# Late attention: gated tiles written over the gates by VectorE and split by GpSimd two maps behind its scaling

## The chip, the cores and the metric

The kernel runs on one core of a Trainium2 chip. The metric is the device time of one execution, in microseconds. A core has five engines that run their own instruction streams and wait for each other by semaphores: TensorE (PE in the profile, with its weight loads as PEld), VectorE (DVE), ScalarE (ACT), GpSimd (POOL) and SyncE (SP, which issues DMAs). TensorE writes to PSUM; GpSimd works on SBUF here.

## The reference

Two transformer blocks follow each other on a sequence of 512 tokens with model width 1024. The first block has windowed and sparse attention, a gated merge and a convolutional feed-forward layer. The change lies in the second block, which mixes three kinds of attention, gates their concatenated output with silu(z), and projects it:

```python
def second_block(x, mem, positions, norm_g, w_in, ...):
    for l in range(DEPTH):
        lam_init = 0.8 - 0.6 * math.exp(-0.3 * l)
        h = rms_norm(x, norm_g[l])
        proj = h @ w_in[l]
        cq, ckv, kr, dq, dk, dv, mq, z = jnp.split(proj, IN_OFFSETS_2, axis=-1)
        y_mla = mla_branch(cq, ckv, kr, positions, ...)      # 8 heads, causal, 64 wide
        y_diff = diff_branch(dq, dk, dv, positions, ...)     # 4 heads, each a difference of two softmaxes
        y_mem = mem_branch(mq, mem, ...)                     # 4 heads over 256 memory tokens
        y = jnp.concatenate([y_mla, y_diff, y_mem], axis=-1) * jax.nn.silu(z)
        x = x + y @ w_out[l]
    return x

# in mla_branch, for a block of 128 queries
sc = jnp.einsum('bqhd,bkhd->bhqk', qblk, k).astype(jnp.float32) * scale
sc = jnp.where(causal_mask(start, s)[None, None], sc, NEG_INF)
p = jax.nn.softmax(sc, axis=-1).astype(v.dtype)
return jnp.einsum('bhqk,bkhd->bqhd', p, v)

# in diff_branch
a = (p[:, :, 0] - lam * p[:, :, 1]).astype(v.dtype)
o = rms_norm(o, subln_g) * (1.0 - lam_init)
```

Everything is float32. The dense products are done as three products of a high part (rounded to the format that TensorE takes at full rate, `fp32r`) and a low part (what the rounding lost): high by high, high by low, low by high. So each operand of a dense product needs a high and a low tile, and this holds for the gated output `y` as well.

## The kernel before

The kernel is one program: projections and the first attention ("ab"), merge, feed-forward layer and its output product, the projections of the second block with their norms, then the late attention, and last the output product `wout2`. Weights arrive in units of 128x1024; for each, ScalarE writes the high part (`stream`, line 731) and GpSimd the low part (`low_half`, line 652).

The late attention works through a list of 20 maps, `LATE`. A map is one softmax matrix of one head (512 queries by its keys) with a place i from 0 to 19:

```text
 0 mla0   1 mla1   2 diff0 hold  3 diff0 sub   4 mla2   5 mla3   6 diff1 hold  7 diff1 sub   8 mla4
 9 diff2 hold  10 diff2 sub  11 mla5  12 diff3 hold  13 diff3 sub  14 mla6  15..18 mem0..mem3  19 mla7
```

Every engine has its own loop over i, and each loop handles several maps in one turn, at different stages. For one map the stages are these.

- TensorE, `scores`: products of queries and keys into PSUM.
- VectorE, `biased` (line 1324): adds the causal mask, copies to SBUF, takes the row minimum. Its inputs are one tile of PSUM and one of SBUF.
- ScalarE (line 889): exponentials with row sums. They need the table of the exponential on ScalarE; another function needs its own table, brought in by a table load instruction.
- VectorE, `normed`: reciprocals of the sums (line 1337), then the rows are scaled, in three groups by 128-query blocks: block 1, blocks 0 and 2, block 3. VectorE scales the first two groups (line 1364). GpSimd scales block 3 of every mla map (`widest`, line 669), half of every mem map (line 715), and all four blocks of a "hold" map (line 709). In a "sub" map VectorE computes the difference with the held map (line 1362), after a small product with lambda (line 1348).
- TensorE, `turn` (line 1987): transposes of the scaled rows, group by group; ScalarE copies them to SBUF (line 864).
- TensorE, `values` (line 2010): products with the values, into PSUM bank 6 or 7 in turn. They wait until the output before the last has left its bank.

For a finished mla or mem map (12 of them, 64 rows by 512 queries each) the end is: VectorE multiplies the output in PSUM by the gate in `FX` and writes it back to PSUM (line 1440, semaphore `y_f`); ScalarE copies that to SBUF, which rounds it to the high part (line 933, `y_hi`); one turn later VectorE subtracts to get the low part (line 1247, `y_lo`). The diff outputs take another way, through a norm over each head: it needs a square root on ScalarE (line 851, which waits for `dm_rin`, VectorE's reciprocal at line 1445), a gating on VectorE (lines 1388 and 1391), a copy on ScalarE (line 917) and the low part on VectorE.

Order on each engine is program order. `wout2` multiplies the eight gated tiles in the order 4, 5, 6, 7, 0, 1, 2, 3 (4 and 5 are diff, 6 mem0 and mem1, 7 mem2 and mem3, 0 to 3 mla), each with its own wait in the first unit.

## Time and profile before

| | |
|---|---|
| median of three runs | 1101.36 us (1101.25 to 1102.08) |
| profiled execution, its own time | 1101.32 us |
| span of the profile | 1099.5 us |
| busy in the span | PE 1050.5, PEld 870.7, DVE 622.8, ACT 550.8, POOL 436.9 us |
| first 950 us | PE busy 919.30 us, granted clock 0.99 |
| 950 to 1052.5 us, the late attention | PE busy 87.41 us, granted clock 0.93 |
| 1052.5 us to the end, `wout2` | PE busy 43.77 of 47.00 us, granted clock 1.00 |

The profile is one execution. Busy time of an engine is the time in which it had an instruction running. The chain of waits is followed back from the last instruction, at each step to what released it; an engine that isn't on it there had time to spare. A timeline gives an engine's instructions by start. Groups by form give, for one line and shape, how often it ran and the mean time of one. A window's row gives busy times with instruction counts, and the granted clock of TensorE, where 1.00 is 2.4 GHz and 0.50 is 1.2 GHz.

### The profile page before, as it was taken

Reading aid. Unit: us, or ns where it says so; the run is one execution under the profiler, and the core shown is the slowest. Engines: PE = TensorE matmul, PEld = TensorE weight load, DVE = VectorE, ACT = ScalarE, POOL = GpSimd, SP = SyncE. Lnnn points to the kernel's source line nnn. Section 1 sums busy time; section 2 is a strip of 40 time slices with the busy share of each in tenths; the row PEclk is TensorE's granted clock in tenths of the full one; section 3 lists DMA queues with packets and bytes.
Section 4 is the critical chain, followed back from the end, with each engine's and each line's share of the span. In section 5 each row is a group of like instructions: output and inputs, shape, how many; then the busy total and the mean of one; then the engine's idle time right before and its main releaser. Section 6 shows DMA issues by size and latency. Waiting matters only on the chain.

```text
span 1099.5 us, 15072 instructions
## 1 busy us (share of the span) xinstructions
PE 1050.5 (96%) x5086; PEld 870.7 (79%) x5086; DVE 622.8 (57%) x1414; ACT 550.8 (50%) x1143; POOL 436.9 (40%) x227
## 2 busy tenths in 40 slices
PE   6999999999999999999999999999999979899798
PEld 3779888799888788888888888778887868766577
DVE  4557376988745466454545455442225989586732
ACT  5443465777634344444444444443344374888831
POOL 2356222233324444444444444414444244444332
PEclk9999999999999999999999999999999999898999
DMA  7564221111013322222223233233353224332123
GB/s 257 186 174 144 74 76 58 58 40 39 29 58 117 128 100 96 96 96 95 100 93 104 93 106 134 96 134 100 112 178 101 77 71 140 98 94 77 49 77 114
DMA packets 38811, 111.87 MB, mean 102 GB/s; under 512 B 5235, under 2 KB 8563, under 8 KB 38067
## 3 DMA queue, kind: packets, MB, share of 16 engines
q1 hardware_dynamic: 28572, 87.60, 24.4%
q10 hardware_dynamic: 8584, 18.89, 5.3%
q0 software_dynamic: 1600, 4.66, 1.1%
q8 instruction: 32, 0.52, 0.2%
q14 instruction: 23, 0.19, 0.1%
HBM read 100.25 MB, written 7.96 MB: 98 GB/s over the span
## 4 chain that ended last, share of the span: by engine, by line
PE 36%; issue 35%; POOL 12%; DVE 8%; ACT 4%; DMA 3%; POOLq 0%; ACTq 0%; DVEq 0%
POOL WLO L652 11%; PE PS L1813 8%; PE PS L1815 8%; PE PS L1814 8%; PE PS L1987 2%; PE PS L2010 2%; DMA RAW<-wstream 2%; PE PS L1901 1%; PE PS L1946 1%; PE PS L1947 1%; DVE PB L1324 1%; ACT PB L889 1%; ACT WHI L731 1%; PE PS L2149 1%; DMA X<-xT 1%
## 5 line engine op out<-in xcount | busy, mean ns | idle before, releaser
L652 POOL TENSOR_TENSOR WLO<-RAW,WHI 128x1024 fp32r<-128x1024 f32 x147 | 355.7, 2420 | 529.1 <-ACT WHI L731 528.8
L731 ACT ACTIVATE WHI<-RAW 128x1024 fp32r<-128x1024 f32 x154 | 162.8, 1058 | 294.4 <-PE PS L1815 273.5
L1813 PE MATMUL PS<-HHI,WHI 128*128 128x512 f32 x648 | 257.4, 397 | 10.6 <-DVE HLO L1225 9.2
L1814 PE MATMUL PS<-HLO,WHI 128*128 128x512 f32 x648 | 254.1, 392 | 0.0
L1815 PE MATMUL PS<-HHI,WLO 128*128 128x512 f32 x648 | 253.9, 392 | 0.0
L1813 PEld LDWEIGHTS PS<-HHI,WHI 128*128 128x128 f32 x648 | 122.9, 190 | 39.9 <-issue 11.7
L1813 PE MATMUL PS<-BHI,WHI 128*128 128x512 f32 x368 | 145.3, 395 | 3.2 <-POOL WLO L652 1.8
L1815 PE MATMUL PS<-BHI,WLO 128*128 128x512 f32 x368 | 143.4, 390 | 0.0
L1815 PEld LDWEIGHTS PS<-HHI,WLO 128*128 128x128 f32 x648 | 122.8, 189 | 26.0
L1814 PE MATMUL PS<-BLO,WHI 128*128 128x512 f32 x368 | 143.3, 389 | 0.0
L1814 PEld LDWEIGHTS PS<-HLO,WHI 128*128 128x128 f32 x648 | 123.0, 190 | 25.4 <-issue 0.8
L1207 DVE TENSOR_TENSOR PS<-PS,PB 128x512 f32<-128x512 f32 x63 | 43.9, 696 | 87.0 <-PE PS L1815 85.4
L1247 DVE TENSOR_TENSOR BLO<-PS,BHI 128x256 fp32r<-128x256 f32 (+4 forms) x140 | 64.8, 508 | 39.4 <-ACT BHI L923 27.9
L1813 PEld LDWEIGHTS PS<-BHI,WHI 128*128 128x128 f32 x368 | 69.1, 188 | 20.4 <-POOL WLO L652 2.5
L889 ACT ACTIVATE PB<-PB,ST 128x256 f32<-128x256 f32 (+4 forms) x164 | 79.4, 500 | 4.8 <-DVE ST L1324 4.7
L1815 PEld LDWEIGHTS PS<-BHI,WLO 128*128 128x128 f32 x368 | 69.1, 188 | 14.8
L1814 PEld LDWEIGHTS PS<-BLO,WHI 128*128 128x128 f32 x368 | 69.1, 188 | 13.8
L1536 DVE SCALAR_TENSOR_TENSOR FX<-PS,CL,FX 128x511 f32<-128x511 f32 (+1 forms) x88 | 61.7, 742 | 12.0 <-ACT FX L983 11.8
L1813 PE MATMUL PS<-WHI,HHI 128*128 128x512 f32 (+2 forms) x128 | 48.5, 379 | 2.7 <-ACT PB L1009 2.0
L1987 PE MATMUL PS<-IDN,PB 128*128 128x128 f32 x270 | 39.3, 284 | 11.5 <-DVE PB L1364 4.8
L1815 PE MATMUL PS<-WHI,HLO 128*128 128x512 f32 (+2 forms) x128 | 48.2, 376 | 0.0
L1814 PE MATMUL PS<-WLO,HHI 128*128 128x512 f32 (+2 forms) x128 | 47.9, 374 | 0.0
(322 smaller groups left out, 1646.0 us busy)
## 6 DMA issues: line engine op xcount, KB each, us to landing
RAW<-wstream SPq DMA_DIRECT2D x154, 512.0 KB, 3.2
X<-xT ACTq DMA_DIRECT2D x4, 512.0 KB, 9.4
BF<-wstream POOLq DMA_DIRECT2D x2, 1024.0 KB, 7.1
BG<-wstream POOLq DMA_DIRECT2D x2, 1024.0 KB, 7.1
bias_b<-bias_rows ACTq DMA_DIRECT2D x2, 1024.0 KB
FX<-bias_b ACTq DMA_DIRECT2D x8, 256.0 KB, 2.8
X<-xT ACTq DMA_DIRECT2D x8, 256.0 KB, 3.6
x_keep<-X ACTq DMA_DIRECT2D x2, 1024.0 KB, 6.1
```

The lines of the kernel that those rows point to most:

```text
L652: pool.tensor_tensor(WLO[:, s, :], RAW[:, s, :], WHI[:, s, :].bitcast(F), ALU.subtract).then_inc(split_lo, 1)
L731: act.activation(WHI[:, c % 2, :], RAW[:, c % 2, :], ACT.Copy).then_inc(split_hi, 1)
L889: ins = act.activation(dst, dst, ACT.Exp, bias=stat(m, NMAX)[:, q:q + 1], scale=-1.0, accum_out=stat(m, SUM)[:, q:q + 1])
L1207: dve.tensor_tensor(PS[:, bank, :], PS[:, bank, :], RSTD, ALU.mult).then_inc(scaled, 1)
L1247: return dve.tensor_tensor(dst_lo, src, dst_hi.bitcast(F), ALU.subtract)
L1324: ins = dve.tensor_tensor_reduce(prob_of(m, q), PS[:, b, o:o + nk], bias_of(m, q), -m["scale"], init, ALU.add, ALU.min, stat(m, NMAX)[:, q ...
L1536: dve.scalar_tensor_tensor(out=y, in0=PS[:, 2 * e + s, 0:SEQ - sh], scalar=cv[:, tap:tap + 1], in1=y, op0=ALU.mult, op1=ALU.add).then_inc( ...
L1813: pe.matmul(dst, a[0], b[0], start=first, stop=False, **kw)
L1814: pe.matmul(dst, a[0], b[1], start=False, stop=False, **kw)
L1815: return pe.matmul(dst, a[1], b[0], start=False, stop=last, **kw)
L1987: ins = pe.transpose(PS[:, 3 + b, o + j * P:o + (j + 1) * P], pr[:, p0:p0 + P], IDN[:, :])
L2010: ins = pe.matmul(PS[:, m["bank"], q0:q1], m["v"](kb), turned_block(m, pt, kb, 0), start=m["first"] and kb == 0, stop=m["last"] and kb == ...
```

## The change

It concerns the 12 mla and mem outputs. In 11 of them, all but the last map mla7 (they are marked `apart`), VectorE still multiplies by the gate, but writes the product over the gate in SBUF instead of back to PSUM. The high and the low part are then made by GpSimd, from that SBUF tile: a `tensor_copy` and a `tensor_tensor` subtraction of 64x512, with a wait between them (`tile_parts`). ScalarE's copy and VectorE's subtraction are gone for the 11. GpSimd does the parts of map i-2 right after its scaling of map i, and those of mem3 at the end. The bank of a map is free for the next output when the gating is done (`y_f`), not when the low part is. The last map keeps the old way under semaphores of its own (`yd`, `yl_hi`, `yl_lo`).

```diff
@@ on the list of maps
                 if maps is LATE and not m.get("diff"):
                     m["yf"] = 1 + len([n for n in maps[:i] if "yf" in n])
+                    m["apart"] = i + 1 < len(maps)
@@ GpSimd
+            def tile_parts(m, done):
+
+                if not m.get("apart"):
+                    return
+                pool.wait_ge(wide_last, len([n for n in LATE[:done] if "latent" in n]))
+                pool.wait_ge(mem_half, len([n for n in LATE[:done] if "pair" in n]))
+                pool.wait_ge(first_held, len([n for n in LATE[:done] if n.get("mode") == "hold"]))
+                pool.wait_ge(ATT["late"]["y_f"], m["yf"])
+                rows, y = m["rows"], FX[m["rows"], m["ztile"], :]
+                pool.tensor_copy(hi(m["ytile"])[rows, :], y).then_inc(yp_hi, 1)
+                pool.wait_ge(yp_hi, m["yf"])
+                pool.tensor_tensor(lo(m["ytile"])[rows, :], y, hi(m["ytile"])[rows, :].bitcast(F), ALU.subtract).then_inc(ATT["late"]["y_lo"], 1)
+                pool.wait_ge(ATT["late"]["y_lo"], m["yf"])
@@ GpSimd, at the end of its turn for map m
                     ins.then_inc(mem_half, 1)
+                if m["i"] >= 2:
+                    tile_parts(LATE[m["i"] - 2], m["i"] + 1)
+            tile_parts(LATE[-2], len(LATE))
             low_halves(UNIT["wout2"] + 2, NPOS)
@@ ScalarE
-                        else:
-                            act.wait_ge(A["y_f"], m["yf"])
-                            act.activation(yt[rows, :], PS[rows, m["bank"], :], ACT.Copy).then_inc(A["y_hi"], 1)
+                        elif not m["apart"]:
+                            act.wait_ge(yd, 1)
+                            act.activation(yt[rows, :], PS[rows, m["bank"], :], ACT.Copy).then_inc(yl_hi, 1)
@@ VectorE
-                    if 0 <= i - 3 < len(maps) and "yf" in maps[i - 3]:
+                    if 0 <= i - 3 < len(maps) and "yf" in maps[i - 3] and not maps[i - 3]["apart"]:
                         m = maps[i - 3]
                         rows = m["rows"]
-                        dve.wait_ge(A["y_hi"], m["y"] + 1)
-                        low_from_psum(lo(m["ytile"])[rows, :], hi(m["ytile"])[rows, :], PS[rows, m["bank"], :]).then_inc(A["y_lo"], 1)
+                        dve.wait_ge(yl_hi, 1)
+                        low_from_psum(lo(m["ytile"])[rows, :], hi(m["ytile"])[rows, :], PS[rows, m["bank"], :]).then_inc(yl_lo, 1)
...
                             dve.wait_ge(A["pv"], m["n"])
-                            dve.tensor_tensor(ps, ps, FX[rows, m["ztile"], :], ALU.mult).then_inc(A["y_f"], 1)
+                            z = FX[rows, m["ztile"], :]
+                            if m["apart"]:
+                                dve.tensor_tensor(z, ps, z, ALU.mult).then_inc(A["y_f"], 1)
+                            else:
+                                dve.tensor_tensor(ps, ps, z, ALU.mult).then_inc(yd, 1)
@@ TensorE, values
                         if not before.get("diff"):
-                            pe.wait_ge(A["y_lo"], before["yf"])
+                            pe.wait_ge(A["y_f"], before["yf"])
...
@@ TensorE, wout2
-                   2: (A["y_lo"], mla[5]["yf"]), 3: (A["y_lo"], mla[7]["yf"])})
+                   2: (A["y_lo"], mla[5]["yf"]), 3: (yl_lo, 1)})
```

Below are three places in the order of instructions, with what each instruction waits for. Line numbers of the kernel after are higher: 709 becomes 725, 669 becomes 671, 715 becomes 731, 851 becomes 870, 889 becomes 908, 1362 becomes 1381, 1364 becomes 1383, 1440 becomes 1461.

GpSimd from the scaling of the first held map (diff0, tile X) on, before; the next two rows are the scalings of block 3 of mla2 and mla3.

```order
L709 TENSOR_SCALAR X<-X,ST 128x384
L709 TENSOR_SCALAR X<-X,ST 128x512
L669 TENSOR_SCALAR PB<-PB,ST 128x512 [waits late_normed]
L669 TENSOR_SCALAR X<-X,ST 128x512 [waits late_normed]
L709 TENSOR_SCALAR PB<-PB,ST 128x128 [waits first_sums]
```

The same place after:

```order
L725 TENSOR_SCALAR X<-X,ST 128x384
L725 TENSOR_SCALAR X<-X,ST 128x512
L690 CAST BHI<-FX 64x512 [waits first_held,late_y_f,mem_half,wide_last]
L692 TENSOR_TENSOR BLO<-FX,BHI 64x512 [waits yp_hi]
L690 CAST BHI<-FX 64x512 [waits first_held,mem_half,late_y_f,wide_last,late_y_lo]
L692 TENSOR_TENSOR BLO<-FX,BHI 64x512 [waits yp_hi]
L671 TENSOR_SCALAR PB<-PB,ST 128x512 [waits late_normed,late_y_lo]
L671 TENSOR_SCALAR X<-X,ST 128x512 [waits late_normed]
L725 TENSOR_SCALAR PB<-PB,ST 128x128 [waits first_sums]
```

The parts of mla0 and mla1, a copy (CAST) and a subtraction each, now stand between the held map and the scaling of mla2.

GpSimd at the end of the late attention before (PB and X hold mem1, mem2 and mem3 in turn, the last row is mla7):

```order
L715 TENSOR_SCALAR PB<-PB,ST 128x256 [waits late_normed]
L715 TENSOR_SCALAR PB<-PB,ST 128x256
L715 TENSOR_SCALAR X<-X,ST 128x256 [waits late_normed]
L715 TENSOR_SCALAR X<-X,ST 128x256
L715 TENSOR_SCALAR PB<-PB,ST 128x256 [waits late_normed]
L715 TENSOR_SCALAR PB<-PB,ST 128x256
L669 TENSOR_SCALAR PB<-PB,ST 128x512 [waits late_normed]
```

and after, from mem1's second scaling on:

```order
L731 TENSOR_SCALAR PB<-PB,ST 128x256
L690 CAST BHI<-FX 64x512 [waits first_held,late_y_f,mem_half,wide_last]
L692 TENSOR_TENSOR BLO<-FX,BHI 64x512 [waits yp_hi]
L731 TENSOR_SCALAR X<-X,ST 128x256 [waits late_normed,late_y_lo]
L731 TENSOR_SCALAR X<-X,ST 128x256
L690 CAST BHI<-FX 64x512 [waits first_held,late_y_f,mem_half,wide_last]
L692 TENSOR_TENSOR BLO<-FX,BHI 64x512 [waits yp_hi]
L731 TENSOR_SCALAR PB<-PB,ST 128x256 [waits late_normed,late_y_lo]
L731 TENSOR_SCALAR PB<-PB,ST 128x256
L690 CAST BHI<-FX 64x512 [waits first_held,late_y_f,mem_half,wide_last]
L692 TENSOR_TENSOR BLO<-FX,BHI 64x512 [waits yp_hi]
L671 TENSOR_SCALAR PB<-PB,ST 128x512 [waits late_normed,late_y_lo]
```

The three pairs of parts are those of mla6, mem0 and mem1; the parts of mem0 stand ahead of mem3's scaling, those of mem1 ahead of mla7's.

ScalarE around the first square root of the diff norm, before (X is a map's exponentials, line 864 copies transposes):

```order
L889 ACTIVATE X,ST<-X,ST 128x512 [waits late_biased]
L933 ACTIVATE BHI<-PS 64x512 [waits late_y_f,late_pv]
L851 ACT_TABLE_LOAD
L851 ACTIVATE PB<-SS 128x512 [waits dm_rin]
L864 ACTIVATE HF<-PS 128x2x128 [waits late_turned,late_pv]
```

and after:

```order
L908 ACTIVATE X,ST<-X,ST 128x512 [waits late_biased]
L870 ACT_TABLE_LOAD [waits dm_rin]
L870 ACTIVATE PB<-SS 128x512 [waits late_pv]
L883 ACTIVATE HF<-PS 128x2x128 [waits late_turned,late_pv]
L883 ACTIVATE HF<-PS 128x128 [waits late_turned]
```

The copy is gone, its wait for `late_pv` has gone on to the square root, and the wait for `dm_rin` now stands ahead of the table load. The same holds at the second square root, six maps later.

## Rows read from the trace of the kernel before

**Rows 1.** Windows: PE, PEld, DVE, ACT, POOL busy, then TensorE clock, DMA, GB/s.

```profile
950.00:1052.50 102.50, 87.41 (x443) 64.10 (x442) 71.73 (x258) 84.77 (x264) 43.28 (x34) 0.93 0.30 82
992.00:996.00 4.00, 4.00 (x12) 2.31 (x11) 0.61 (x3) 3.20 (x13) 3.29 (x4) 0.61 0.44 105
```

**Rows 2.** Chain of waits (start us, us, what): first passage, and its repetition.

```profile
966.88 1.55 DVE PB L1362 x4
...
968.74 0.67 DVE BLO L1247
...
972.04 0.36 DVE PB L1364
...
972.49 1.79 POOL PB L669
...
974.98 2.16 PE PS L2010 x8
...
989.61 1.78 POOL X L669
...
992.32 3.62 PE PS L2010 x8
```

**Rows 3.** Timeline of GpSimd (start us, us, line, operation): the first held map.

```profile
962.20 4.27 POOL L709 TENSOR_SCALAR X<-X,ST 128x128 f32<-128x128 f32 x4 [1.69 <-DVE ST L1335]
```

**Rows 4.** Groups by form on GpSimd: xcount, busy us, mean ns of one.

```profile
L652 POOL TENSOR_TENSOR WLO<-RAW,WHI 128x1024 fp32r<-128x1024 f32 x147 | 355.7, 2420 | 529.1 <-ACT WHI L731 528.8
...
L709 POOL TENSOR_SCALAR PB<-PB,ST 128x512 f32<-128x512 f32 x3 | 4.7, 1567 | 0.0
...
L641 POOL TENSOR_SCALAR_AFFINE_SELECT TRI<-TRI 128x512 f32<-128x512 f32 x1 | 0.6, 603 | 0.0
```

**Rows 5.** Timeline of GpSimd and VectorE in the first dense stage.

```profile
397.89 2.40 POOL L652 TENSOR_TENSOR WLO<-RAW,WHI 128x1024 fp32r<-128x1024 f32 x1 [2.98 <-ACT WHI L731]
...
398.69 2.14 DVE L1190 SCALAR_TENSOR_TENSOR HLO<-X,CL,HHI  x1 [1.14 <-ACT HHI L745]
```

**Rows 6.** Groups by form on VectorE: the same operation at the start.

```profile
L1225 DVE SCALAR_TENSOR_TENSOR HLO<-X,CL,HHI 128x512 fp32r<-128x512 f32 x8 | 5.7, 749 | 3.0 <-ACT HHI L764 3.0
```

**Rows 7.** Timeline of VectorE, three instructions of the late attention.

```profile
1002.76 0.20 DVE L1445 RECIPROCAL SS<-SS 128x8 f32<-128x8 f32 x1
...
1014.18 0.16 DVE L1348 TENSOR_TENSOR ST<-ST,LAM 128x4 f32<-128x4 f32 x1
...
1032.86 0.20 DVE L1445 RECIPROCAL SS<-SS 128x8 f32<-128x8 f32 x1
```

**Rows 8.** Timeline of ScalarE: two loads of the root table, one copy.

```profile
1002.28 1.28 ACT L851 ACT_TABLE_LOAD   x1
...
1031.73 1.28 ACT L851 ACT_TABLE_LOAD   x1
...
1038.80 0.63 ACT L917 ACTIVATE BHI<-PB 128x512 fp32r<-128x512 f32 x1 [0.59 <-DVE PB L1391]
```

**Rows 9.** Chain of waits, later in the late attention, up to its end.

```profile
1012.24 4.28 POOL PB L709 x4
...
1018.61 0.71 DVE PS L1440
...
1020.94 0.36 DVE X L1364
...
1040.07 0.68 DVE PS L1440
...
1042.51 0.63 DVE PB L1364 x2
...
1043.22 1.83 POOL PB L715 x2
...
1048.57 1.72 PE PS L2010 x4
...
1050.29 2.42 PE PS L2010 x8
```

More of the change, by code:

```diff
@@ L227, in build @@
         first_sums, first_held, mem_half = sem("first_sums"), sem("first_held"), sem("mem_half")
+        yp_hi, yl_hi, yl_lo, yd = sem("yp_hi"), sem("yl_hi"), sem("yl_lo"), sem("yd")
         late_hi, late_lo = sem("late_hi"), sem("late_lo")
@@ L928, in attention @@
                             if m["h"] % 2:
-                                act.wait_ge(A["y_hi"], m["y"] + 1)
+                                act.wait_ge(A["y_hi"], m["h"] + 1)
                                 act.activation(YSQ, YT, ACT.Square).then_inc(dm_sq, 1)
-                        else:
-                            act.wait_ge(A["y_f"], m["yf"])
-                            act.activation(yt[rows, :], PS[rows, m["bank"], :], ACT.Copy).then_inc(A["y_hi"], 1)
+                        elif not m["apart"]:
+                            act.wait_ge(yd, 1)
+                            act.activation(yt[rows, :], PS[rows, m["bank"], :], ACT.Copy).then_inc(yl_hi, 1)
             attention("ab")
@@ L2002, in values @@
                         else:
-                            pe.wait_ge(A["y_hi"], y - 1)
+                            pe.wait_ge(A["y_hi"], before["h"] + 1)
                 if m["first"] and name == "ab" and y > 8:
```

## The prediction

> **What bounds the kernel now.** I read the windows first. In the late attention (950 to 1052.5 us) TensorE is busy for 87.41 of 102.50 us, no other engine for more, and GpSimd for only 43.28 [rows 1]: TensorE waits for some 15 us, and nobody is full. So the chain of waits decides, and only this stage is touched. In the chain the reader should see one passage twice, 17.12 us apart (972.49 and 989.61) [rows 2]: VectorE's four subtractions of a sub map (L1362), the low part of an output (L1247), its gating and the next masks, its scaling (L1364), then GpSimd's scaling of block 3 (L669), then TensorE. Behind it the chain goes over ScalarE (L917), GpSimd's scaling of the held map diff3, VectorE and GpSimd again [rows 9]. GpSimd is idle most of the time, but its scalings are links of this chain; whatever is queued ahead of one can move the end.
>
> **Prices.** VectorE loses a subtraction of 0.67 us per output [rows 2]; the gating stays (0.71) [rows 9]. GpSimd gets 11 copies and 11 subtractions of 64x512, which the trace doesn't have. Its subtraction takes 2.42 us at 1024 columns [rows 4]; half is 1.21, and with a fixed part it is more. I take 1.3. The copy lies between 0.60 (one input, one output, 512 columns) and 1.57 (a scaling of 512 columns with its scalar) [rows 4]; it is nearest to the first, so I take 0.8, bounds 0.6 and 1.57. With 0.15 for two waits one pair is p = 2.3 us, from 1.9 to 3.1. The page GPSIMD Engine Reference of the Trainium skill (Performance versus the Vector engine) has 0.77 us measured for a one-input loop over 512 elements; by it the sum below would be 5.1 us instead of 5.2.
>
> **Who blocks whom.** In the first dense stage a VectorE instruction with two SBUF inputs started 0.80 us into GpSimd's subtraction (397.89 to 400.29) and took 2.14 us [rows 5]; the same operation takes 0.75 alone [rows 6]. It ended at 400.83, half a microsecond behind GpSimd: it stood until GpSimd was through. But L1348, also with two SBUF inputs, took its 0.16 us at 1014.18 [rows 7] in the middle of GpSimd's scaling (1012.24 to 1016.52) [rows 9]. So I count a GpSimd subtraction as closing the port to VectorE's L1362 and L1364, a scaling or a copy as not. The masks and the gating read one operand from PSUM; I take them as free.
>
> The Trainium skill (SBUF — State Buffer, Who interferes with whom) makes it broader: a VectorE instruction with two SBUF inputs waits for any GpSimd instruction that reads SBUF. L1348 speaks against that for scalings. By that rule the copies would hold L1362 too, 0.35 us more in each of two passages: 0.7 us on the sum.
>
> **The sum, by places of the chain.**
>
> Passage A. GpSimd ends the held map at 962.20 + 4.27 = 966.47 [rows 3]; mla0 is gated by then. Copy 966.55 to 967.35, subtraction from 967.45, which reads from about 967.65. L1362 runs 966.88 to 968.8 in four pieces. The subtraction gets in between two pieces and the rest stands until about 968.9 to 969.3: L1362 ends at 969.85, a microsecond late. The low part is gone (0.67 back), so mla1 is gated at 970.6. Its copy runs to 971.45, its subtraction 971.55 to 972.9. VectorE's L1364, before at 972.04, is 0.45 late at 972.5, and stands until 972.9. The scaling of block 3 starts at 973.25 instead of 972.49: **+0.76**. Hiding place of the pair of mla0: none, L1362 is beside it.
>
> Passage B has the same distances: **+0.76**.
>
> Square root 1. Before, the table load started at 1002.28, ahead of the reciprocal (1002.96), so the root ran at 1003.57 [rows 7, 8]. The order of instructions after has the wait for the reciprocal ahead of the load. Then: 1002.96 + 0.04 + 1.28 = 1004.3, and the chain stays with ScalarE from the root up to its copy L917, which the held map diff3 at 1012.24 waits for [rows 9]: **+0.74**. The removed ScalarE copy gives nothing here. The pair of mla4 has GpSimd to itself.
>
> Passage C. The held map and L1362 have no pair beside them, since mla5 is gated only behind them, 1018.61 + 0.71 = 1019.32 [rows 9]. Then copy to 1020.15, subtraction to 1021.6; L1364, due at 1020.94, stands until about 1021.55 and the scaling follows at 1021.95 to 1022.0: **+0.62**.
>
> From 1023 to 1037 us TensorE is the chain; the pair of mla6 fits beside it. Removed low parts and TensorE's shorter waits for a bank are off the chain here.
>
> Square root 2. The reciprocal is ready at 1033.06; the load then begins 1.33 us later than before (1031.73) [rows 7, 8], and the exponentials behind it are as late. L917 had 0.59 us of slack [rows 8]: **+0.72**.
>
> End. mem0's gating ends at 1040.07 + 0.68 + 0.72 = 1041.47 [rows 9]. Subtraction 1042.45 to 1043.8; L1364, due at 1042.51 + 0.72 = 1043.23, stands until 1043.8, and mem3's scaling starts at 1044.45, not 1043.22. It ends at 1046.3; the pair of mem1 comes next, to 1048.6; only then mla7's scaling, to 1050.2. Four transposes to 1050.9, the values of mem3 (1.72) to 1052.6, and the values of mla7 start there instead of 1050.29 [rows 9]: 2.3 us, of which 0.72 are counted: **+1.6**. mem3's parts are ready near 1055.8, its tile is needed near 1056.8: hidden, with 1 us to spare. Behind that, `wout2` is TensorE's alone and only shifts.
>
> Sum: 0.76 + 0.76 + 0.74 + 0.62 + 0.72 + 1.6 = 5.2 us. The profiled execution took 1101.32 us (span 1099.5), the median is 1101.36: they are one number. **Forecast 1106.5 us.** With the short copy and 1.2 for the subtraction the terms are 0.5, 0.5, 0.74, 0.35, 0.72, 1.0: 3.8 us, 1105.2. With 1.57: 0.6, 0.6, 0.74, 1.3, 0.72, 3.1: 7.1 us, 1108.4.
>
> **Rivals.**
> 1. The clock. In passage B the values took 3.62 us for eight matmuls, in A 2.16 [rows 2]; in that window the granted clock was 0.61 of 2.4 GHz, so part of it at 1.2 GHz [rows 1]. It fell after TensorE had stood idle several times. The change lengthens such gaps, in A above all, by 0.76 us. One more dip costs 1.46: 1108.0. Against it: passage C has gaps and kept full clock.
> 2. The load isn't held. If the root table is loaded before the wait after all, square root 1 gives 0.57 back instead of losing 0.74, and square root 2 costs nothing: 5.2 - 1.31 - 0.72 = 3.2 us, 1104.5. The listed order speaks against it.
> 3. The port isn't closed, since 64 rows or 512 columns might slip through. Then A and B gain the 0.67 us of the low part each, C costs about 0.2, the end about 1.0, square roots 1.46: +1.3 us, 1102.7. The 2.14 us of rows 5 speak against it.
> 4. The other side. GpSimd has 59 us idle in the stage, and VectorE's chain in A and B is 0.67 us shorter each. If the port stays open and the load runs ahead of its wait, that decides: -1.34 - 0.57 + 0.2 + 1.0 = -0.7 us, 1100.7. It turns into a gain only if p stays under about 2.9 us, so that mla1's pair (from 969.45) ends before the scaling at 972.49.
>
> **How the numbers follow.** Forecast 0.50 (with both copy prices), clock 0.20, load not held 0.13, port open 0.11, the other side 0.06. The likeliest is 1106.5, its own range 1105.2 to 1108.4. Eight in ten: from below case 2 to above a dip with the long copy, 1103.0 to 1109.5. A measurement here can tell 0.2%, 2.2 us. Above 1103.56 lie the forecast, the clock and nearly all of case 2: slower 0.82. Within: case 3, the rest of case 2 and a third of case 4: 0.14. Faster: 0.04.
>
> **What would show it.** Right: L1381 (was L1362) takes 3 us instead of 1.94 in A and B, with one piece near 1.9; L1383 has single pieces far over 0.4; GpSimd goes from a low-part subtraction straight into the scaling of mla2, mla4, mla6, mem3 and mla7, with nearly no idle; the table loads start behind the reciprocal; TensorE waits for GpSimd before mla7's last transposes. Wrong: copies above 1.6 or subtractions under 1.1 us, L1381 at 1.94, a table load that starts with the copy's old place, or `wout2` waiting for mem3's low part.

## The result, and the profile after

The kernel after takes 1110.36 us (median of 4 runs, 1109.68 to 1110.92) against 1101.3 us: ratio 1.0077, 95% interval 1.006 to 1.0095. The forecast was 1106.5 us and its range ended at 1109.5: the sign was right, the loss was larger. In a later set of runs the same kernel gave 1.0051 (1.0031 to 1.0070; single runs from 1102.2 to 1109.6 us). By the ratios the loss is 8.5 us in the first set and 5.6 us in the second (there 3.7 us by the medians, 1104.92 against 1101.2); the two intervals share 1.0060 to 1.0070.

Windows of the kernel after (busy times, granted clock, DMA, GB/s), against [rows 1]:

```profile
950.00:1062.00 112.00, 94.46 (x446) 68.42 (x445) 67.99 (x249) 81.79 (x254) 63.38 (x56) 0.88 0.27 75
975.70:979.10 3.40, 3.33 (x8) 1.99 (x9) 1.20 (x6) 2.17 (x9) 1.80 (x2) 0.50 0.26 63
1045.40:1049.50 4.10, 0.00 (x0) 0.00 (x0) 3.79 (x14) 3.39 (x12) 1.88 (x2) 1.00 0.00 0
1050.80:1057.60 6.80, 5.77 (x15) 3.58 (x16) 1.41 (x3) 1.21 (x4) 4.77 (x5) 0.50 0.38 153
```

The late attention grew by 9 us and its granted clock fell from 0.93 to 0.88; `wout2` keeps full clock. Two stretches at 0.50 (1.2 GHz) are new: one right behind passage A, one at the end, behind 4.1 us in which TensorE did nothing at all.

Prices of the new work, GpSimd's groups by form; then its timeline in passage A, against [rows 2, 3]:

```profile
L692 POOL TENSOR_TENSOR BLO<-FX,BHI 64x512 fp32r<-64x512 f32 x11 | 14.0, 1276 | 0.9
L690 POOL CAST BHI<-FX 64x512 fp32r<-64x512 f32 x11 | 6.7, 609 | 22.1 <-DVE FX L1461 21.4 <-POOL X L725 0.2 <-POOL PB L725 0.2
```

```profile
967.07 0.60 POOL L690 CAST BHI<-FX 64x512 fp32r<-64x512 f32 x1 [0.23 <-POOL X L725]
967.76 1.28 POOL L692 TENSOR_TENSOR BLO<-FX,BHI 64x512 fp32r<-64x512 f32 x1
...
973.94 1.78 POOL L671 TENSOR_SCALAR PB<-PB,ST 128x512 f32<-128x512 f32 x1 [0.32 <-DVE PB L1383]
```

A pair takes 0.61 + 0.08 + 1.28 = 1.97 us, not 2.3. VectorE beside it, in A and in B:

```profile
967.37 0.32 DVE L1367 TENSOR_TENSOR ST<-ST,LAM 128x4 f32<-128x4 f32 x1
967.73 3.04 DVE L1381 SCALAR_TENSOR_TENSOR PB<-PB,ST,X 128x256 f32<-128x256 f32 x4
...
987.06 3.20 DVE L1381 SCALAR_TENSOR_TENSOR PB<-PB,ST 128x256 f32<-128x256 f32 x4
```

L1381 takes 3.04 and 3.20 us instead of 1.94, as foreseen. ScalarE's root tables, against [rows 8]:

```profile
1007.30 1.28 ACT L870 ACT_TABLE_LOAD   x1 [3.25 <-DVE SS L1468]
1008.60 0.63 ACT L870 ACTIVATE PB<-SS 128x512 f32<-128x512 f32 x1
...
1038.69 1.28 ACT L870 ACT_TABLE_LOAD   x1 [2.17 <-DVE SS L1468]
```

Both loads start behind the reciprocal. TensorE at the end (start, us), against [rows 9], and GpSimd's scaling of mla7:

```profile
1049.56 0.63 PE L2010 MATMUL PS<-IDN,PB 128*128 128x128 f32 x4 [4.17 <-DVE PB L1383]
1051.83 1.11 PE L2010 MATMUL PS<-IDN,PB 128*128 128x128 f32 x4 [1.64 <-POOL PB L731]
1052.74 3.62 PE L2033 MATMUL PS<-HF,BF 128*128 128x512 f32 x4
1056.15 1.96 PE L2010 MATMUL PS<-IDN,PB 128*128 128x128 f32 x10
```

```profile
1053.96 1.56 POOL L671 TENSOR_SCALAR PB<-PB,ST 128x512 f32<-128x512 f32 x1
```

The values of mem2 take 3.62 us where full clock gave 1.88. The scaling of mla7, late as it is, ends at 1055.52, before TensorE comes to its transposes. The same place in the kernel before, where the granted clock was 1.00 throughout:

```profile
1039.51 1.95 PE L2010 MATMUL PS<-HF,BF 128*128 128x512 f32 x4 [1.38 <-DVE BLO L1247]
1043.23 0.63 PE L1987 MATMUL PS<-IDN,PB 128*128 128x128 f32 x4 [1.77 <-DVE PB L1364]
1045.10 0.65 PE L1987 MATMUL PS<-IDN,PB 128*128 128x128 f32 x4 [1.25 <-POOL PB L715]
1045.59 1.88 PE L2010 MATMUL PS<-HF,BF 128*128 128x512 f32 x4
```

The first row is the values of mem1: they waited 1.38 us for a low part to leave their bank, and then TensorE waited 1.77 us for the first scaled rows of mem3. After, the values of mem1 start at 1043.51 without a wait, and both waits are one of 4.17 us.

**Where the time went.** For each kernel I took the starts of GpSimd's scalings from the start of mla0's scaling, and subtracted those of the kernel before; "first product" is the first matmul of `wout2`. The rows are increments in us, so a column adds up to the delay of `wout2`. "Filled" are two variants, e9 and e8 below, in which TensorE transposes something useless while it would wait.

| stretch | forecast | after | after, repeated | filled after less filled before |
|---|---|---|---|---|
| A: to mla2's scaling | 0.76 | 1.07 | 1.32 | 0.83 |
| to the held map diff1 | 0 | 1.61 | 0.00 | -0.01 |
| B: to mla4's scaling | 0.76 | 0.76 | 0.76 | 0.76 |
| to mla5's scaling | 0 | 0.52 | -1.04 | 1.32 |
| root 1: to the held map diff3 | 0.74 | 0.84 | 0.83 | 1.27 |
| C: to mla6's scaling | 0.62 | 0.34 | 0.35 | 0.39 |
| to mem2's scaling | 0 | 0.11 | 0.10 | 0.09 |
| root 2: to mem3's scaling | 0.72 | 0.78 | 0.78 | 0.80 |
| End: to the first product | 1.6 | 2.86 | 2.10 | 0.61 |
| sum | 5.2 | 8.9 | 5.2 | 6.1 |

The forecast's 1.6 for the end has about 0.5 us in it that it put ahead of mem3's scaling (1044.45 instead of 1043.22, with 0.72 of that counted for root 2); by places it is 1.2 in the row of root 2 and 1.1 in that of the end, so the end missed by more than its row shows, and mem3's scaling came sooner than forecast.

In the first profile 0.38 us ahead of mla0's scaling and 0.33 us behind the last product make it up to the 9.6 us between the spans; the products of `wout2` themselves take TensorE 43.80 us in both, at full clock. The last column is told below.

### The profile page after: what moved, and what is told of

The parts are those of the page before. It is cut to its first block and busy times, and to the rows that moved or that the text cites. A ratio compares the mean times of both kernels' runs of the same rounds, so it can differ in the third digit from the quotient of the medians.

```text
span 1109.1 us, 15094 instructions
## 1 busy us (share of the span) xinstructions
PE 1059.9 (96%) x5086; PEld 877.6 (79%) x5086; DVE 618.7 (56%) x1403; ACT 547.2 (49%) x1132; POOL 457.6 (41%) x249
## 5 line engine op out<-in xcount | busy, mean ns | idle before, releaser
L1266 DVE TENSOR_TENSOR BLO<-PS,BHI 128x256 fp32r<-128x256 f32 (+4 forms) x129 | 57.3, 492 | 38.1 <-ACT BHI L942 27.6
L2010 PE MATMUL PS<-IDN,PB 128*128 128x128 f32 x270 | 42.3, 298 | 14.9 <-DVE PB L1383 7.2
L2010 PEld LDWEIGHTS PS<-IDN,PB 128*128 128x128 f32 x270 | 33.7, 153 | 23.8 <-DVE PB L1383 7.7
```

What stands on the lines that cost most here:

```text
L1266: return dve.tensor_tensor(dst_lo, src, dst_hi.bitcast(F), ALU.subtract)
L2010: ins = pe.transpose(PS[:, 3 + b, o + j * P:o + (j + 1) * P], pr[:, p0:p0 + P], IDN[:, :])
```

## The experiments

"Ratio" is against the kernel before on the same chip. All edits are to the kernel after unless said otherwise.

**e16: the same kernel again.** 

> The kernel after once more, unchanged, for an interval on the same chip: ratio 1.006 to 1.0095 as measured before. If it comes out at 1.005 or 1.006, the forecast was nearer than the first four runs say, and the clock term is smaller.

Ratio 1.0051 (1.0031 to 1.0070). The profiled run took 1102.16 us, the lowest of its six (median 1104.92). The spans of the two profiles of this one kernel differ by 8.9 us: 5.2 us of that is there already at mla0's scaling (956.47 and 951.32 us), ahead of everything that the change touches, and 3.7 us lies between there and `wout2`. In passage A:

```profile
961.92 0.60 POOL L690 CAST BHI<-FX 64x512 fp32r<-64x512 f32 x1 [0.23 <-POOL X L725]
962.61 1.26 POOL L692 TENSOR_TENSOR BLO<-FX,BHI 64x512 fp32r<-64x512 f32 x1
```

```profile
963.38 0.52 DVE L1367 TENSOR_TENSOR ST<-ST,LAM 128x4 f32<-128x4 f32 x1
963.93 1.94 DVE L1381 SCALAR_TENSOR_TENSOR PB<-PB,ST,X 128x256 f32<-128x256 f32 x4
```

Here TensorE was still at 0.50 from 952.5 to 959.1, VectorE came later, and only the small product L1367 stood until the subtraction ended at 963.87. Whether the port or the clock held it, A lost about the same. The 1.61 us behind A is absent. The end has its stretch again:

```profile
1041.20:1047.90 6.70, 5.24 (x12) 2.87 (x13) 2.15 (x6) 1.82 (x6) 5.58 (x5) 0.50 0.58 196
```

**e1: the table loads freed.**

```diff
-                        act.wait_ge(A["pv"], m["n"])
+                        if not m.get("apart"):
+                            act.wait_ge(A["pv"], m["n"])
```

> The kernel after, with ScalarE no longer waiting for the values of a map whose parts GpSimd makes; in the listed order the root table's load then has no wait and stands ahead of the one for the reciprocal. Theory (the held load is 1.3 us at each of two square roots, both on the chain): loads start right behind the exponentials (near 1004.1 and 1036.5), the roots right behind the reciprocals (1007.3 and 1038.7), and the kernel ends 2 to 2.6 us sooner than the kernel after (1110.4): 1107.8 to 1108.4. Rival (the held loads lie beside the waits for GpSimd and cost nothing): under 0.5 us, 1110. Rival clock: if the shorter wait also spares TensorE a stretch at half clock, up to 1.5 us more, 1106.3.

Ratio 1.0050 (1.0031 to 1.0070). ScalarE:

```profile
1002.99 1.28 ACT L870 ACT_TABLE_LOAD   x1
1006.17 0.63 ACT L870 ACTIVATE PB<-SS 128x512 f32<-128x512 f32 x1 [1.90 <-DVE SS L1469]
```

By the trace root 1 falls from +0.84 to -0.49, root 2 from +0.78 to +0.15: 1.96 us together. So the orphaned wait, not the new work, held the loads. Against the repeated kernel after (1.0051) the times don't show it; the pair e9 and e11 gives 0.0024, 2.6 us, though their intervals still overlap.

**e2 and e3: without parts, with copies alone.** e2 drops both instructions of `tile_parts` and lets `wout2` wait for the gating (`y_f`) in their place; e3 drops the subtraction. So e2 computes neither part of the 11 outputs, and e3 no low part.

> The kernel after without GpSimd's copies and subtractions: the high and low parts of 11 outputs are left out (stale data is multiplied in their place), all else as in the kernel after. It gives the price of the parts with everything that they drag along. Theory (GpSimd's parts in front of its scalings and beside VectorE's subtractions are the loss, with the clock behind them): what stays is two held table loads (+0.74, +0.72) less the low part that VectorE has lost in passages A and B (-0.67 each): near the kernel before, 1101 to 1102.5. Rival (writing the gated output to SBUF, or TensorE running ahead of the banks, makes the loss): it stays above 1106. The clock: if the parts' waits bring the additional half-clock stretches, the granted clock of the late attention goes back to 0.93; if they come from TensorE's other pattern, it stays at 0.88.

> The kernel after with GpSimd's 11 copies (high parts) but without its 11 subtractions (the low parts of 11 outputs are left out, stale data stands in their place). Theory (a subtraction closes the port to VectorE's instructions with two SBUF inputs, a copy does not): VectorE's four subtractions of a sub map take 1.94 us again, the scaling of mla7 waits for one copy, and the time is that of the kernel without parts plus 0.5 to 1 us, 1102 to 1103. Rival (any GpSimd instruction that reads SBUF closes it): the small product with lambda takes 0.32 and the four subtractions 2.3 us or more, 0.5 us later in A and in B than without parts. Rival (what counts is GpSimd's time in front of its scalings, whoever blocks whom): a third of the loss that the parts make remains, about 1104.

e2 1.0008 (0.9997 to 1.0019), e3 1.0016 (1.0002 to 1.0029): taken together, the gating in SBUF, the earlier bank and ScalarE's lost copy cost nothing that can be told; the parts do. In e3:

```profile
964.99 0.61 POOL L690 CAST BHI<-FX 64x512 fp32r<-64x512 f32 x1 [0.23 <-POOL X L723]
```

```profile
965.16 2.18 DVE L1379 SCALAR_TENSOR_TENSOR PB<-PB,ST,X 128x256 f32<-128x256 f32 x4
```

2.18 us instead of 1.94: a copy holds VectorE too, by 0.24 us, which I had denied. The Trainium skill (SBUF — State Buffer, Who interferes with whom) says that a VectorE instruction with two SBUF inputs contends with any GpSimd instruction that reads SBUF; here copy and subtraction both agree with it, the scaling of [rows 7] doesn't.

e2 also shows the other half. Up to mla7's scaling it is 1.12 us ahead of the kernel before, at the first product 1.89 behind. TensorE there:

```profile
1043.91 0.63 PE L2003 MATMUL PS<-IDN,PB 128*128 128x128 f32 x4 [4.02 <-DVE PB L1376]
1046.10 1.12 PE L2003 MATMUL PS<-IDN,PB 128*128 128x128 f32 x4 [1.56 <-POOL PB L727]
```

The kernel before waited 1.38 us, worked 1.95 us, then waited 1.77 us, at full clock. Freed from the bank, TensorE does the values of mem1 at once and waits 4 us in one piece, without any parts on GpSimd; then four transposes take 1.12 us instead of 0.65.

**e4: TensorE's waits filled.** The added code, in `turn`:

```diff
+                    if A is ATT["late"] and WARM.get(m["i"], {}).get(g):
+                        if m["t_free"][g]:
+                            pe.wait_ge(A["p_hi"], m["t_free"][g])
+                        b, o = m["place"][qs[0]]
+                        for _ in range(WARM[m["i"]][g]):
+                            pe.transpose(PS[:, 3 + b, o:o + P], IDN[:, :], IDN[:, :])
```

> The kernel after with 79 extra transposes of 128x128 on TensorE (into PSUM places that the next true transposes overwrite), put where it waits in the trace: 20 before mla0's second group, 5 each at mla2, mla4, diff3, mla6, 28 and 8 at mem3, 8 at mla7. Nothing else changes. Theory (the loss beyond my 5.2 us is TensorE at 1.2 GHz behind its waits, about 3.8 us): granted clock of the late attention above 0.93, values in A and B 2.2 us instead of 3.5 to 4.0, and 1106 to 1107; lower still if the stretch at 965 us, which the kernel before has too, goes away. Rival (the dips don't hang on the waits, or cost nothing on the chain): clock stays at 0.88 and the time is 1110 to 1112, with the extra transposes in the way.

(The places add up to 84, not 79.) Ratio 1.0043 (1.0027 to 1.0060). The dip behind A and the one at the end are gone (the trace reaches the first product 2.4 us sooner than after's first one), but 20 transposes stood behind mla0's first group instead of ahead of it, where the wait of 3.04 us is, and delayed the first held map by 2.3 us. The later fillings put them ahead.

**e8 and e9: both kernels filled.** e8 is the kernel before, e9 the kernel after.

> The kernel before with the same extra transposes (12 instead of 22 at mem3's first group). It is the control to the other filled kernels: what the filling alone brings. Theory (half clock costs only where TensorE is the chain behind it: the 3.62 us against 2.16 us in passage B): 1 to 2 us less, ratio 0.998 to 0.999. Rival (the transposes get in the way, or the clock falls in any case): 1.000 to 1.002. Should it come out as fast as the kernel with placed parts, free loads and filling, the change has nothing of its own to give.

> The kernel after with TensorE's waits filled at the same places as in the filled kernel before, 28 transposes at mem3's first group (92 in all). With the clock at full speed in the late attention on both sides, the difference to the kernel before with filling (ratio 0.9972) is what the waits alone cost. Theory (the prediction's sum of waits was about right and only the clock was missing): 5.2 to 5.6 us above it, ratio 1.0019 to 1.0023. Rival (the waits were undersized too): 7 us or more above it, 1.0036 or more.

(86 transposes in the full filling of e7, 76 in e8, 92 in e9.) e8 0.9972 (0.9961 to 0.9984), e9 1.0037 (1.0023 to 1.0051). Windows of e8, then of e9, from 950 us to the first product:

```profile
950.00:1047.30 97.30, 87.31 (x502) 65.73 (x500) 69.14 (x248) 81.26 (x261) 40.81 (x33) 1.00 0.30 82
```

```profile
950.00:1057.60 107.60, 97.05 (x539) 72.89 (x538) 68.50 (x251) 81.40 (x255) 63.28 (x56) 0.97 0.29 78
```

Filling takes 3.1 us off the kernel before by the times (1.9 us by the traces, from mla0's scaling on), which I had underrated, and 4.4 us off the kernel after as first measured, 1.5 as repeated. What remains between them is 0.0065, some 7 us, uncertain by 2; by the traces 6.1 us to the first product. So the ratio is the rival's (1.0036 or more), not the 1.0019 to 1.0023 of the theory. But e9 kept a stretch at half clock behind mla4 (the 1.32 of the table) which e8 had not, and a second near 1016 us that no row of the table shows. Without the first the waits add up to 4.7 us, near the forecast's 5.2. The 0.61 of the end is small because of the filling: in e8 six transposes at mla7 stand in TensorE's way, and make its end 0.38 us longer than before's; against the unfilled kernel before, e9's end costs 0.99 us.

**e10 and e11: one term each, filled.** e10 puts the parts of mem0 to mem3 behind mla7's scaling, e11 frees the loads.

> The filled kernel after with the parts of mem0 to mem3 behind the scaling of mla7. At full clock it prices the last term by itself. Theory (pairs ahead of the scalings of mem3 and mla7 delay the end by 1.6 us): 1.6 us less than the filled kernel after, ratio lower by 0.0015; from mem3's scaling to mla7's 2.2 us instead of 4.3. Rival (TensorE's own work covers the later scaling, as it did at half clock): under 0.7 us, 0.0006.

> The filled kernel after with the table loads not held (22 instead of 28 transposes at mem3, since the wait there is shorter). Theory (1.3 us at the first root, 0.6 to 0.7 us at the second, both on the chain also at full clock): 2.0 us less than the filled kernel after, ratio lower by 0.0018. Rival (at full clock TensorE arrives sooner, waits elsewhere and the loads are hidden): under 0.7 us.

e10 1.0022 (1.0009 to 1.0034), e11 1.0013 (0.9998 to 1.0028), against 1.0037. By the traces, from mla5's scaling to the first product, e11 gains 2.00 us on e9: as expected. e10 starts mla7's scaling 2.2 us sooner after mem3's, yet from mem3's scaling to the first product gains only 0.30 us (0.54 with the 0.24 by which mem3's scaling itself is sooner). That looks like the rival's case, but the filling is in the way. TensorE in e10:

```profile
1053.04 0.82 PE L1998 MATMUL PS<-IDN 128*128 128x128 f32 x6
1053.69 0.60 PE L2019 MATMUL PS<-IDN,PB 128*128 128x128 f32 x4
```

mla7's scaling had ended at 1051.66; the six useless transposes in the first row delay the true ones by 0.65 us. e10's end is 0.69 us over before; e12 and e18 (below), with the same four pairs behind mla7's scaling and no transposes there, are 0.05 and 0.04 us over. So at full clock moving the pairs away is worth about 1 us of the end, not 0.30. e10's time came down by 0.0015, with overlapping intervals.

**e5: the end's pairs moved, not filled.**

```diff
-                if m["i"] >= 2:
+                if 2 <= m["i"] < 17:
                     tile_parts(LATE[m["i"] - 2], m["i"] + 1)
-            tile_parts(LATE[-2], len(LATE))
+            for n in LATE[15:19]:
+                tile_parts(n, len(LATE))
```

> The kernel after, with the parts of mem0 to mem3 all behind the scaling of mla7 on GpSimd; everything up to mla6's parts stays. Theory of the prediction (the pairs of mem0 and mem1 delay the scalings of mem3 and mla7, 1.6 us, by the trace after 2.2 us from mem3's to mla7's scaling): 1.6 to 2.8 us less than the kernel after, a ratio to before of 1.0053 to 1.0062. Theory of the clock (from 1051 us on TensorE works at half clock and is itself the chain; the scaling of mla7 ended at 1055.5, TensorE came to its transposes only at 1056.15): the scaling of mla7 moves forward by 2 us and the first product of the last stage by 0.5 us only; ratio 1.0070 to 1.0075. The half-clock stretch of 6.8 us behind TensorE's idle time of about 4 us at mem3's first group stays.

Ratio 1.0049 (1.0030 to 1.0068): 3.1 us under the first result, nothing that can be told under the repeated one, and in neither theory's range. The trace decides:

```profile
1046.65 1.56 POOL L671 TENSOR_SCALAR PB<-PB,ST 128x512 f32<-128x512 f32 x1
```

```profile
1047.63 3.62 PE L2034 MATMUL PS<-HF,BF 128*128 128x512 f32 x4
1051.05 1.30 PE L2011 MATMUL PS<-IDN,PB 128*128 128x128 f32 x10
```

mla7's scaling ends at 1048.21, TensorE at half clock gets to it at 1051.05. From mem3's scaling to the first product: 2.20 us over before, with the pairs in their old place 2.10 (repeated) and 2.86 (first).

**e13, e14, e15: the end's clock.** e13 adds 28 and 8 transposes at mem3's two groups only; e15 does so without parts; e14 adds `pe.wait_ge(dm_lo, 2)` ahead of the values of mem1.

> The kernel after with 28 and 8 extra transposes at mem3's two groups and nowhere else. Theory (the half-clock stretch behind the 4.2 us wait stretches the last values, transposes and the start of the last stage): no such stretch at the end, the values of mem2 take 1.9 us instead of 3.6, and the time is 1.5 to 2.2 us under the kernel after: ratio to before lower by 0.0014 to 0.0020. The stretches in A and B stay as they are. Rival (GpSimd's scaling of mla7 sets the end, whatever the clock): under 0.5 us.

> The kernel after; only the values of mem1 on TensorE wait, besides, for the low part of the second diff tile, as late as they waited for a low part in the kernel before. TensorE then waits 2.8 us, works 1.9 us and waits 1.3 us, instead of 4.2 us in one piece. No work is added. Theory (one long wait lowers the clock, the same wait in two parts does not): no half-clock stretch at 1051, 1.2 to 2 us less than the kernel after. Rival (the sum of the waits counts, or 2.8 us is already too long): the stretch stays or starts earlier, time within 0.5 us of the kernel after or above.

> The kernel after without GpSimd's copies and subtractions (high and low parts of 11 outputs left out) and with mem3's waits filled by 28 and 8 transposes. Without filling this kernel was 1.1 us ahead of the kernel before at the scaling of mla7 and 1.9 us behind at the first product of the last stage. Theory (those 3.0 us are the half-clock stretch): they go, ratio 0.998 instead of 1.0008. Rival (they are TensorE's own backlog): 1.0005 or more.

e13 1.0045 (1.0030 to 1.0060). TensorE:

```profile
1047.60 1.88 PE L2041 MATMUL PS<-HF,BF 128*128 128x512 f32 x4
...
1050.86 0.66 PE L2018 MATMUL PS<-IDN,PB 128*128 128x128 f32 x4 [0.71 <-POOL PB L671]
```

Now the values take 1.88 us and TensorE does wait for mla7's scaling, 0.71 us. From mem3's scaling to the first product it costs 0.98 instead of 2.10 us. The time doesn't resolve that: 0.0006 under e16 of the same set, where 0.0014 to 0.0020 was expected. So at full clock the pairs are worth about 1 us here, and at half clock they hide behind the 1.1 us and more that the clock takes.

e15 0.9995 (0.9985 to 1.0005) against e2's 1.0008; from mla7's scaling to the first product its trace has 0.1 us over before, e2's 3.0. That the idle time before it brings the slow stretch, and that the stretch costs the 3 us, is shown by the traces; the times give back 1.4 us of it, half of what was expected.

e14 gave 1.0048 (1.0034 to 1.0061), no gain on e16. TensorE waited 2.76 us and the clock fell all the same, only sooner:

```profile
1040.70 3.75 PE L2035 MATMUL PS<-HF,BF 128*128 128x512 f32 x4 [2.76 <-ACT HF L883]
...
1046.68 1.95 PE L2035 MATMUL PS<-HF,BF 128*128 128x512 f32 x4
```

Since it also rose sooner, the values of mem2 (second row) are nearly at full speed, and its trace comes to the first product 1.4 us sooner than e16's; the times don't show it. e14 doesn't restore the waits of before, 1.38 and 1.77 us: its own wait is twice the first of them. But it bears on what counts. It stood idle for 2.76 us in all before its clock fell; the kernel before stood for 3.15 us, in two pieces, at full clock.

**e6, e7, e12, e17, e18: towards a better kernel.** e7 is e6 with e1's edit and filling, e12 and e18 the same with less filling (76 transposes), e17 the kernel before with that filling, but 12 instead of 24 transposes at mem3's first group (64 in all). In e6 GpSimd does the parts at these maps, and at a sub map only after VectorE has normed it:

```diff
+            PARTS_AT = {3: (0,), 7: (1,), 10: (2, 3), 11: (4,), 16: (5, 6), 19: (7, 8, 9, 10)}
...
-                if m["i"] >= 2:
-                    tile_parts(LATE[m["i"] - 2], m["i"] + 1)
-            tile_parts(LATE[-2], len(LATE))
+                if m.get("mode") == "sub":
+                    pool.wait_ge(ATT["late"]["normed"], m["n0"] + len(m["groups"]))
+                for k in PARTS_AT.get(m["i"], ()):
+                    tile_parts([n for n in LATE if "yf" in n][k], m["i"] + 1)
```

> The kernel after with GpSimd's parts at other places: mla0's and mla1's after VectorE has done the subtractions of the first and the second sub map, mla2's and mla3's after those of the third, mla4's after the scaling of mla5, mla5's and mla6's after that of mem1, mem0's to mem3's after that of mla7. All work is done, the table loads are still held. Theory (the parts cost only by their place: beside VectorE's subtractions and ahead of GpSimd's scalings): VectorE's subtractions take 1.94 us, and the time is that of the kernel without parts, ratio 1.000 to 1.002. Rival (22 GpSimd instructions cost wherever they are, through the SBUF port or the power that lowers the clock): 1.004 or more.

> As the parts placed elsewhere, and besides the table loads not held (ScalarE no longer waits for the values of maps split by GpSimd), and TensorE's waits filled with 81 extra transposes (18 at mla0's first group, 4 to 5 at the sub maps, at mla2, mla4 and mla6, 22 and 7 at mem3, 6 at mla7). Theory (three terms add up: placing, held loads about 2 us together, clock dips about 3 us at the end and one in passage B): 3 to 5 us under the kernel before, ratio 0.995 to 0.9975. Rival (the terms overlap, one chain takes over from the other): within 0.2% of before.

> Parts placed elsewhere, loads not held, and filling only where the trace still shows a wait at that place: 22 at mla0, 5 each at mla2, mla4, diff3 and mla6, 24 and 10 at mem3, none at mla7 nor the other sub maps (76 in all). Theory (in the fuller version TensorE was itself the chain at mla7, 0.7 us of transposes in its way): 0.5 to 1 us less than it, ratio 0.9970 or below. Rival (the few percent of idle time elsewhere need the filling, the clock falls once more): 0.998 to 1.000, with a half-clock stretch in the trace.

> The kernel before with the filling of the best kernel: 22 transposes at mla0, 5 each at mla2, mla4, diff3 and mla6, 12 and 10 at mem3 (12 instead of 24, since its wait there is in two parts), none at mla7 (64 in all). Theory (the six transposes at mla7 were in TensorE's way): 0.3 to 0.6 us less than with the first filling, ratio 0.9967 to 0.9972. Rival: a stretch at half clock comes back and it is 0.998 or more.

> The best kernel again (parts placed elsewhere, loads not held, filled), beside the kernel before with the same filling. Theory (two low parts of 0.67 us less in VectorE's chain of passages A and B, and TensorE not waiting for banks; by the traces 1 to 1.5 us): ratio lower than its neighbour's by about 0.001, 0.9957 to 0.9965. Rival (the change gives nothing of its own): the same ratio within 0.0005 or a higher one.

e6 1.0012 (1.0001 to 1.0023), all four L1381 groups at 1.94 us: with every part computed, it is as fast as the kernel without parts. e7 0.9978 (0.9965 to 0.9992), e12 0.9961 (0.9945 to 0.9976), e18 0.9968 (0.9955 to 0.9982), e17 0.9971 (0.9954 to 0.9987). Windows of e17, then of e18:

```profile
950.00:1051.80 101.80, 91.15 (x515) 68.18 (x514) 72.85 (x264) 86.12 (x267) 43.26 (x34) 1.00 0.31 83
```

```profile
950.00:1049.30 99.30, 91.58 (x518) 69.68 (x518) 65.03 (x247) 80.61 (x254) 62.23 (x54) 0.98 0.31 84
```

e12 and e18 are one kernel, 4.3 and 3.5 us under the kernel before, and so under both given ones. But the kernel before with the same filling is as fast within what can be told: by the traces e18 reaches the first product 1.1 us sooner, and gives 0.6 us of it back in `wout2` (47.6 instead of 47.0 us). What can be told from the kernel before is the filling, not the change.

## Why the prediction was right in direction and short in size

**Right.** The port: L1381 stood until the subtraction ended, B cost 0.76 in every kernel that had the pairs there, A 0.83 at undisturbed clock (forecast 0.76 each). The held load: 0.84 and 0.78 (forecast 0.74 and 0.72), and e1 and e11 undo it. C was 0.34 instead of 0.62, because a pair takes 1.97 us, not 2.3, and VectorE's scaling was slowed there, not stopped:

```profile
1026.08 1.19 DVE L1383 TENSOR_SCALAR X<-X,ST 128x256 f32<-128x256 f32 x3
```

It took 1.19 instead of 0.88 us. In the repeated profile the total up to `wout2` is 5.2 us, as forecast; that is luck in good part, since larger losses in A (1.32) and at the end (2.10) and a gain of 1.04 behind mla4 offset each other, in the lowest run of six. The kernel before had its own half-clock stretch there (the 3.62 us of [rows 2]); e8, without it, gains 1.26 at the same place.

**The step that failed** is "Removed low parts and TensorE's shorter waits for a bank are off the chain here", written of 1023 to 1037 us and carried on to the end, whose 1.6 us has no term for the bank; and with it a sum that had the clock at zero. Releasing the bank early moves the values of mem1 out of a wait and joins 1.38 and 1.77 us of waiting into 4.2. Each unfilled trace with that wait in one piece (after, e16, e1, e2, e3, e5, e6) shows a half-clock stretch behind it; before has none (the wait is 3.53 us in e1, 4.0 to 4.2 in the others). That makes the term of the end 2.1 to 2.9 us instead of 1.6, and its content is another: about 1 us of waiting for GpSimd, the rest clock (e13, e15). The sign that the prediction named for this term, TensorE waiting for GpSimd ahead of mla7's last transposes, is in neither profile of the kernel after; it appears only where the end is filled (0.71 us in e13). That idle time brings the stretch is shown by filling it; that the bank is what joined the two waits is read from the traces, since no run gives them back as they were.

Rival 1 named the clock, with 0.20, but as one dip in A. In the first profile there is one behind A (1.61 us, against 1.46 worked out), a longer one behind B (0.52) and the one at the end. Forecast plus these is 5.2 + 1.61 + 0.52 + 1.26 (end) + 0.31 (A) = 8.9; the rest cancels. It was a compound of forecast and rival 1, and I had priced them apart.

**Also wrong**: that a copy doesn't hold VectorE (e3: 0.24 us); that nothing but L1381 and L1383 is held, while the small product L1367 took 0.32 us beside a copy and 0.52 beside a subtraction instead of 0.16. Both are small.

**Open**: why the dip behind A came in one profile and not in the other. The gaps around it differ by tenths of a microsecond, and TensorE's slow stretch ahead of it ended later in the repeat. Also open is why the first result (1.0077) and the repeat (1.0051) differ. More than half of the difference between their two profiles, 5.2 of 8.9 us, lies ahead of mla0's scaling, where the change has no part; over all the traces here that start moves between 951.3 and 957.8 us.

## What to carry to other kernels

A wait taken off TensorE need not shorten its idle time: add up what stands before and behind it, and if two waits join into one as long as those here, price the stretch behind it at 1.2 GHz as part of the forecast, not as a rival. Work that fills a wait must not stand where TensorE is late already: six such transposes took 0.65 us in e10. Work handed to GpSimd is priced by its neighbours on VectorE and by the scaling queued behind it; the same 22 instructions cost 4.7 us or more in one order (after against e2), and nothing that can be told in another (e6 against e2). When an instruction is removed, look for the wait it carried and where that now stands.

## What the runs showed of the hardware

A GpSimd subtraction of 64x512 (1.28 us) holds VectorE's 128x256 and even its 128x4 instruction with two SBUF inputs until it ends, a copy (0.61 us) by 0.24 us; a VectorE scaling with one tensor input was slowed by 0.31 us (C). Yet in the middle of GpSimd's scalings of a held map (128x128 to 128x512) the 128x4 product took 0.16 us [rows 7], and 0.22 us at the same place in e6.

TensorE's clock costs this kernel without any change about 3 us: 76 transposes whose results nobody reads make the kernel before 0.28% faster (0.9961 to 0.9984). In the late attention of these traces every unfilled wait of TensorE of 2.76 us or more (up to 4.17) has a stretch at a granted clock of 0.50 behind it, and the waits of 1.38 and 1.77 us of the kernel before have none. But a long wait isn't needed: before also ran at 0.57 from 1005 to 1009 us, behind waits of 0.88 and 0.30 us.

One unchanged program differed by 5.4 us in its median between two sets of runs, more than the whole gain or loss of most edits here; only runs made together should be compared closely.
